# Strassen over 12 instead of 8 of the 16 chunks of an input projection, with the reloaded sums of x

## The chip, the cores and the metric

One core of one Trainium2 chip runs the kernel. The metric is the device time of one execution in microseconds (us). In the kernel text PE is TensorE, DVE is VectorE (`nc.vector`), ACT is ScalarE (`nc.scalar`), POOL is GpSimd, SP is SyncE, which here only issues DMAs.

## The reference, cut to what matters

One layer of a hybrid attention encoder in float32, for 16 meta tokens, 512 new frames of a prompt and 64 frames of a running stream (592 tokens, D_MODEL 2048):

```python
z = einsum('bld,dc->blc', h, w_in)            # h: 592 x 2048, w_in: 2048 x (52 tiles of 128 columns + 16 forget columns)
fox group: softmax(q k^T * SCALE + c_q - c_k, causal) v       # 16 heads, c is the running sum of log-sigmoid(forget gate)
swa group: sliding-window softmax with relative bias and a sink, 16 query heads on 4 key heads
out = concat(fox * silu(fg), swa * silu(sg)) @ w_out          # 2048 x 2048
y = layer_norm(ALPHA * x + out)
```

All keys, values and log forget values are outputs as well. The 52 column tiles of the input projection are the longest part of the kernel, and the change is in it.

## The kernel before, in words

**Precision.** Each float32 operand is split into a high part (a copy by ACT to float32r) and a low part (raw minus high, by DVE). A product of one 128-row chunk of the contraction is three matmuls: high x high, high x low, low x high. `xh`, `xl` hold x split once; `wh`, `wl` hold the split weights of the two tiles in work.

**Duos.** A duo is two column tiles (f = 0, 1) times two halves of the tokens (h = 0 `early`, h = 1 `late`, 296 tokens each; for gate and query tiles the first half is 280, as the meta tokens are left out). That is four results of 16 chunks each. The first tile pair ("v", "g") is projected plainly while x arrives (`opening_products`); then come duos 1 to 25. For the first `2 * CUT` chunks a duo is a 2 x 2 block product done in Strassen's way with seven block products instead of eight (`block_product`), each of `CUT` chunks; the remaining chunks are done plainly (`plain`). `CUT` is 4: seven block products of 4 chunks and eight plain units of 4 chunks, all in `UNITS` = 15 units of 12 matmuls (`unit`, u = 0 to 14). Every unit counts up `unit_done`. Banks TOP, BOTTOM and SIDE collect the products; DVE forms the results from them and from `first_part`, `diff_part`, `mid_part`, `last_part` (`take_six`, `take_seven`, `take_five`, `join`), ACT's `keep_first` frees TOP after unit 0.

**Sums.** The block products need sums of weight blocks, made for every duo by DVE (`make_seven`, `make_five`, `make_six`, `make_four`, each followed by a split into high and low: `seven_part`, `five_part`, `six_part`, `right_part`, `four_part`), and three sums of x blocks, made once in `opening_splits` (L1378 to L1382) and kept in SBUF split in high and low: `sum7`, `sum6`, `sum3`. `x21 - x22` is made in place at L1393. `front_parts` splits the FRONT (the first `2 * CUT` chunks) of tile 0, `back_parts` the BACK of either tile.

**Stretches.** `whole` writes the order out: a first duo alone; stretches of two duos ("vg", "qk") for each pair of fox heads; two longer stretches at the start of the two halves of the swa group; six short stretches of one duo ("gq"); and a final stretch in which the output projection (`out_step`) begins. While the duos of one pair are projected, the attention of the pair before is spread over the same steps s: `score_at`, `turn_at`, `value_at` of `Stretch` say before which step PE issues the five query tiles' scores, transposes of the probabilities, and products with the values. DVE handles `scores` at the same s and `reciprocals` two steps later, ACT `probabilities` one step later, `scale_rows` two later and `keep_turned` one after the transposes. `out_at` is where `gate_heads` (L1343) multiplies by the gates, `v_at` where the values of the next pair are transposed (`turn_values`, `keep_values`), `cached_at` where the cached keys are split. Every engine runs its own copy of this loop in order, so an instruction that waits holds up all that stands behind it on that engine.

**In the first duo** DVE also computes the forget gates: `gate_inputs`, `gate_ones`, `gate_reciprocals` (s = 3), `gate_logs` (s = 5), `gate_sums` (s = 7, the running sums, `c_ready`). PE's `turn_gates` transposes them behind unit GATES_TURNED_AT = 11, DVE's `keep_gates` reads them at s = 10 (the loop variable, after which PE's `turn_values` at s = V_FIRST_AT = 14 may overwrite the bank; it waits on `cq_ready`).

**Loads.** SP loads the weights of the next duos as FRONT and BACK pieces of both tiles (`load_part`, L596), 512 KB each, each as soon as DVE has made the low parts of what it overwrites. The POOL queue loads the row terms `cbc` (L728, L782), the cached keys and values, and stores the outputs and the finished pairs.

Of the kernel before, what the change touches and what calls it, by code (L numbers as in the profile page):

```python
# [24 lines left out]
F32 = mybir.dt.float32  # L25
# [39 lines left out]
UNITS = 15  # L65
DUOS = PROJ_TILES // 2
CUT = KO // 4
CUT_LEN = CUT * P
HALF = TOK // 2
GATES_TURNED_AT, V_FIRST_AT = 11, 14  # L70
GATE_ROWS = 80
BIAS_COPIES = FOX_PAIRS
RAW = 12
MIX_PARTS = [(0, 2), (2, 5), (5, 8), (8, 12), (12, 14)]
# [46 lines left out]
class Fox(Values):  # L121
# [31 lines left out]
    @staticmethod  # L153
    def metas(g, i):
        return 4 * g + i + 1


class Swa(Values):
# [32 lines left out]
    @staticmethod  # L191
    def metas(g):
        return 4 * FOX_PAIRS + g - FOX_PAIRS + 1
# [8 lines left out]
class Stretch:  # L202
# [8 lines left out]
    def __init__(self, duos, d0=None, own=None, pair=None, kv=None, kind=None, g=None, kvs=None,  # L211
# [5 lines left out]
        self.steps = OUT_STEPS if final else UNITS * len(duos)  # L217


        if final:  # L220
            score = [2 * i + 1 for i in range(5)]
        elif len(duos) == 2:
            score = [3 * i + 3 for i in range(5)]
        else:
            score = [2 * i + 1 for i in range(5)]
        turn = [x + 4 for x in score]
        value = [turn[2], turn[2], turn[4], turn[4], score[4] + 5 if len(duos) < 2 else score[4] + 7]
        self.score_at, self.turn_at, self.value_at = score, turn, value
        self.out_at = None if kind is None or keep else value[-1] + 2
        self.before_at = 0 if final else 2  # L230
        self.v_at = None
        if kv is not None:
            self.v_at = value[-1] + 3 if kind else V_FIRST_AT
        self.cached_at = self.steps - 5
# [55 lines left out]
def build(nc, xT, w_all, w_ff, b_f, lf_cache, k_cache, v_cache, sinks, rel, keep_k, keep_v,  # L290
          x_p, x_s, ln_g, ln_b, y_p, y_s, fkT, fvT, lf_out, skT, svT, kept_k, kept_v):
    ctx = ExitStack()
    with ctx:
# [10 lines left out]
        def sem(name):  # L304
# [8 lines left out]
        sum7_high, sum7_low, sum6_high, sum6_low, sum3_high, sum3_low = (  # L313
            sb(f"sum{n}", [P, CUT, HALF], F32R) for n in ("7_high", "7_low", "6_high", "6_low", "3_high", "3_low"))


        raw7, raw6, raw3 = (sb(f"raw{n}", [P, CUT, HALF], F32, at=sums_at + 4 * CUT * HALF * (2 * i + 1))
                            for i, n in enumerate((7, 6, 3)))
# [52 lines left out]
        gate_terms = sb("gate_terms", [P, 5, HALF], F32, at=keys_at)  # L371
        z, e, u1, wk, az = (gate_terms[0:GATE_ROWS, i, :] for i in range(5))
# [3 lines left out]
        cT = sb("cT", [N_HEADS, C_LEN], F32, at=keys_at + 5 * TOK * 4)  # L376
# [32 lines left out]

        c_rows = nc.dram_tensor("c_rows", [N_HEADS, C_LEN], F32, kind="Internal").ap()  # L410
        rel_rows = nc.dram_tensor("rel_rows", [N_HEADS, REL], F32, kind="Internal").ap()
        rel_copies = nc.dram_tensor("rel_copies", [N_HEADS, P, REL], F32, kind="Internal").ap()
# [12 lines left out]
        z_cleared = sem("z_cleared")  # L425
# [1643 lines left out]
```

## Time and profile before

| | |
|---|---|
| median of 3 runs | 1018.45 us (1018.03 to 1019.0) |
| profiled execution, its own time | 1019.1 us |
| its span in the profile | 1017.6 us |
| opening (x arrives, first pair "v", "g") | 0 to 39.25 us |
| duos 1 to 25 | 39.25 to 795.7 us |
| output projection and layer norm | to 1017.6 us |
| PE busy | 998.6 us (98%) |
| DVE busy | 715.2 us (70%) |
| ACT busy | 531.7 us (52%) |
| DMA | 115.06 MB, mean 113 GB/s |

The time of an execution is its span and some 1.5 us around it. "Busy" of PE is the union of overlapping matmuls (each shown as some 0.3 us although one follows another after about 0.14 us), so the pace is read from start times. The duos begin, in the timeline of PE, at 39.25 (duo 1), 67.29, 102.17, 129.91, 161.94, 189.68 and 221.62 us (duo 7); duo 18, the first short one, runs from 550.5 to 581.9, duo 19 to 613.4 us. In the rows of busy time by stretch the columns are: stretch, its length, busy time (and instructions) of PE, PEld, DVE, ACT and POOL, PE's granted clock, share of the DMA engines, GB/s. In a timeline row the first two numbers are start and duration.

### The profile page before, as it was taken

To read this page: it belongs to the slowest core of one execution; us is meant where nothing else is said; L and a number is where in the kernel's file an instruction comes from. 1 tells how busy PE (TensorE), PEld (TensorE's weight loads), DVE (VectorE), ACT (ScalarE), POOL (GpSimd) and SP (SyncE) were. 2 spreads that over 40 slices of the span, in tenths; PEclk is the share of its full clock that TensorE was granted. 3 is DMA by queue.
4 is the path that set the end of the run, shared out by engine and by line. 5 is a ranking of instruction groups with operands and counts; after the bars stand their busy time and mean duration, and the time that the engine had idled before them with its cause. 6 is when DMAs were issued, how large, how long until landed. Compare 5 with 4: busy or idle time off the path is not lost.

```text
span 1017.6 us, 20277 instructions
## 1 busy us (share of the span) xinstructions
PE 998.6 (98%) x7283; PEld 937.3 (92%) x7283; DVE 715.2 (70%) x1423; ACT 531.7 (52%) x1217; POOL 81.5 (8%) x156
## 2 busy tenths in 40 slices
PE   9999999999999999999999999999999999999995
PEld 6899999999999999999999999999999888888884
DVE  6988686776868677686767787668787655141685
ACT  5556465565645556464655676556677562111400
POOL 1620101001010100001010000000000000000000
PEclk9999999999999999999999999999999999999998
DMA  9142333223233323234321222231226443222423
GB/s 347 57 134 100 117 112 130 90 96 108 94 125 110 126 67 103 98 106 140 111 95 60 91 81 98 98 105 56 85 82 249 173 175 104 83 82 82 166 68 118
DMA packets 36258, 115.06 MB, mean 113 GB/s; under 512 B 9312, under 2 KB 9728, under 8 KB 33584
## 3 DMA queue, kind: packets, MB, share of 16 engines
q1 hardware_dynamic: 24208, 87.00, 24.8%
q0 software_dynamic: 11856, 27.14, 7.9%
q8 instruction: 31, 0.51, 0.2%
q10 hardware_dynamic: 144, 0.26, 0.1%
q14 instruction: 19, 0.16, 0.1%
HBM read 99.31 MB, written 18.29 MB: 116 GB/s over the span
## 4 chain that ended last, share of the span: by engine, by line
PE 86%; DVE 6%; DMA 4%; issue 2%; ACT 2%; SPq 1%; DVEq 0%; ACTq 0%
PE ps L1642 28%; PE ps L1652 25%; PE ps L1895 20%; PE ps L1860 5%; PE ps L1834 4%; DMA w_raw<-in_w_all 2%; PE ps L1818 2%; PE ps L1817 2%; DMA x_raw<-in_xT 2%; DVE wl L1118 1%; DVE tb L1295 1%; PE ps L1880 1%; SPq L582 0%; PE ps L1838 0%; ACT pt L961 0%
## 5 line engine op out<-in xcount | busy, mean ns | idle before, releaser
L1642 PE MATMUL ps<-xh,wh 128*128 128x296 f32 (+1 forms) x860 | 258.8, 301 | 0.2 <-DVE xl L1366 0.2
L1642 PE MATMUL ps<-xh,wl 128*128 128x296 f32 (+1 forms) x860 | 254.8, 296 | 0.0
L1642 PE MATMUL ps<-xl,wh 128*128 128x296 f32 (+1 forms) x860 | 254.6, 296 | 0.0
L1895 PE MATMUL ps<-wh,mix_parts 128*128 128x512 f32 x576 | 184.1, 390 | 0.0
L1642 PEld LDWEIGHTS ps<-xh,wh 128*128 128x128 f32 x860 | 161.8, 188 | 3.8 <-DVE xl L1366 1.8
L1642 PEld LDWEIGHTS ps<-xl,wh 128*128 128x128 f32 x860 | 161.9, 188 | 0.0
L1642 PEld LDWEIGHTS ps<-xh,wl 128*128 128x128 f32 x860 | 161.5, 188 | 0.0
L1118 DVE TENSOR_TENSOR wl<-w_raw,wh 128x1024 fp32r<-128x1024 f32 (+1 forms) x150 | 143.0, 953 | 19.8 <-ACT wh L853 8.5
L939 ACT ACTIVATE tb<-tb,small 128x256 f32<-128x256 f32 (+5 forms) x160 | 81.3, 508 | 92.2 <-DVE small L1314 64.2
L1895 PEld LDWEIGHTS ps<-wh,mix_parts 128*128 128x128 f32 x576 | 108.2, 188 | 22.3
L1895 PE MATMUL ps<-wl,mix_parts 128*128 128x512 f32 x320 | 124.5, 389 | 0.0
L1652 PE MATMUL ps<-xh,wh 128*128 128x296 f32 x400 | 121.4, 304 | 2.0 <-ACT first_part L891 1.4
L1652 PE MATMUL ps<-xl,wh 128*128 128x296 f32 x400 | 119.2, 298 | 0.0
L1652 PE MATMUL ps<-xh,wl 128*128 128x296 f32 x400 | 119.1, 298 | 0.0
L1652 PE MATMUL ps<-sum_high,wh 128*128 128x296 f32 x300 | 92.1, 307 | 1.2 <-DVE kT L1224 1.2
L1652 PE MATMUL ps<-sum_high,wl 128*128 128x296 f32 x300 | 89.7, 299 | 0.0
L1652 PE MATMUL ps<-sum_low,wh 128*128 128x296 f32 x300 | 89.6, 299 | 0.0
L1114 DVE TENSOR_TENSOR wl<-w_raw,wh 128x1024 fp32r<-128x1024 f32 x32 | 38.1, 1222 | 68.9 <-ACT wh L841 68.8
L1652 PEld LDWEIGHTS ps<-xh,wh 128*128 128x128 f32 x400 | 75.2, 188 | 2.6 <-ACT first_part L891 1.6
L951 ACT ACTIVATE tb<-tb,small 128x256 f32<-128x256 f32 (+4 forms) x160 | 71.7, 495 | 9.8 <-DVE small L1329 9.8
L1652 PEld LDWEIGHTS ps<-xl,wh 128*128 128x128 f32 x400 | 75.4, 189 | 0.0
L1652 PEld LDWEIGHTS ps<-xh,wl 128*128 128x128 f32 x400 | 75.2, 188 | 0.0
(198 smaller groups left out, 1737.3 us busy)
## 6 DMA issues: line engine op xcount, KB each, us to landing
w_raw<-in_w_all SPq DMA_DIRECT2D x106, 512.0 KB, 4.5
w_raw<-in_w_all SPq DMA_DIRECT2D x14, 1024.0 KB, 4.8
cbc<-c_rows POOLq DMA_DIRECT2D x16, 360.0 KB, 4.1
x_raw<-in_xT SPq DMA_DIRECT2D x7, 592.0 KB, 11.7
rows<-in_x_p POOLq DMA_DIRECT2D x4, 1024.0 KB, 5.2
out_y_p<-rows SPq DMA_DIRECT2D x16, 256.0 KB, 2.5
mix_rows<-mixT POOLq DMA_DIRECT2D x14, 288.0 KB, 2.4
rel_copies<-rel_rows POOLq DMA_DIRECT2D x8, 384.0 KB, 10.5
```

The costliest lines, as they stand in the source:

```text
L939: nc.scalar.activation(t, t, ACT.Exp, bias=nm, accum_out=total[:, i % 3, head:head + 1]).then_inc(exp_done, 1)
L951: nc.scalar.activation(row, row, ACT.Copy, scale=recip[:, i % 3, head:head + 1]).then_inc(scaled, 1)
L1114: nc.vector.tensor_tensor(wl[slot][:, a], w_raw[slot % 2][:, a], wh[slot][:, a].bitcast(F32), ALU.subtract).then_inc(w_low, 1)
L1118: nc.vector.tensor_tensor(low, raw, high.bitcast(F32), ALU.subtract).then_inc(done, 1)
L1295: ins = nc.vector.scalar_tensor_tensor(out=rows_[:, head, a:b], in0=st.score_out(ps, head, piece, b - a), scalar=cqp[:, i, head:head + 1], ...
L1642: ins = nc.tensor.matmul(ps[:, bank, result(tile, h)], a[f][:, w], b[:, ko, first:first + width], start=(ko == n_first and i == 0), stop=( ...
L1652: ins = nc.tensor.matmul(ps[:, bank, 0:HALF], a[:, w], b[:, j, :], start=(start and j == 0 and i == 0), stop=(stop and j == CUT - 1 and i ...
L1817: nc.tensor.matmul(out, queries, k2[:, head, a:b], start=True, stop=False)
L1818: ins = nc.tensor.matmul(out, queries, k_low[:, head, a:b], start=False, stop=True)
L1834: ins = nc.tensor.transpose(st.turn_out(ps, head, j), tb[:, i % SLOTS, head, first:first + P], ident[:])
L1860: ins = nc.tensor.matmul(ps[head_rows(head), bank, at:at + q], v_nat[:, block_, HD * head:HD * head + HD], moving[:, head, 0:q], start=(j ...
L1895: ins = nc.tensor.matmul(ps[:, bank, :], a, b[slot][:, w], start=(ko == 0 and i == 0), stop=(ko == KO - 1 and i == len(products) - 1))
```

## The change

- `CUT` is 6: Strassen covers 12 chunks, and `REST` = 2 chunks remain for each plain unit. The steps of a duo are 29 pieces of 2 chunks (6 matmuls) instead of 15 units of 4 chunks; `unit_done` still counts 15 per duo. The plain units of result (0, 1) now stand ahead of those of (1, 0): units 9 and 10 are (0, 1), units 11 and 12 are (1, 0).
- The sums of x are half as large again, and only `sum7` stays in SBUF. `sum6` and `sum3` share the tile `sum_both` (1776 KB, high and low). Both are stored in DRAM once in the first duo (`sum_rows`) and each is loaded again for each duo: `sum6` when unit 7 is done, `sum3` when unit 1 is done. `sum3` is now made in place of x11 in `x_raw`, and split in the first duo by `last_sum`.
- FRONT of a tile is 768 KB, BACK 256 KB; the weight sums are 768 columns.
- Scores in a stretch of two duos stand at pieces 10, 16, 22, 28, 34 (before, in units: 3, 6, 9, 12, 15); in a short one at 1, 5, 9, 13, 17 (units 1, 3, 5, 7, 9). ACT and DVE follow with a lag of 2 and 4 pieces. Transposes come 8 pieces after the scores.
- Several steps of ACT and DVE move, `back_parts(d, 0)` of DVE from the end of the duo before to piece 2, the join of (1, 0) to piece 27. In the first duo the gates' steps stand at s = 14, 14 and 18, `turn_gates` at 25, `keep_gates` at 26, `turn_values` at 28.
- The copies of the bias rows in DRAM are made for 32 instead of 128 rows, and read in four DMAs instead of two.

```diff
+UNIT_PIECES = [3, 3, 3, 3, 1, 1, 3, 3, 3, 1, 1, 1, 1, 1, 1]
+PIECES = sum(UNIT_PIECES)
-CUT = KO // 4
+CUT = 3 * KO // 8
+REST = (KO - 2 * CUT) // 2
-GATES_TURNED_AT, V_FIRST_AT = 11, 14
+GATES_TURNED_AT, V_FIRST_AT = 25, 28
...
-            score = [3 * i + 3 for i in range(5)]
+            score = [6 * i + 10 for i in range(5)]
         else:
-            score = [2 * i + 1 for i in range(5)]
-        turn = [x + 4 for x in score]
+            score = [4 * i + 1 for i in range(5)]
+        self.lag = 1 if final else 2
+        turn = [x + 4 * self.lag for x in score]
...
@@ sync @@
             for f in range(2):
-                sp.wait_ge(w_low, f + 1)
+                sp.wait_ge(w_low, f + 3)
                 load_part(1, f, FRONT, front_loaded)
             for f in range(2):
-                sp.wait_ge(w_low, f + 3)
                 load_part(1, f, BACK, back_loaded)
+            sp.wait_ge(sum_low, 2)
+            sp.dma_start(sum_rows[0], sum_both[:].rearrange("p a b c -> p (a b c)")).then_inc(sums_stored, 16)
             sp.wait_ge(back_low[0], 1)
             load_part(2, 0, BACK, back_loaded)
+            sp.wait_ge(sum_low, 4)
+            sp.dma_start(sum_rows[1], sum_both[:].rearrange("p a b c -> p (a b c)")).then_inc(sums_stored, 16)
+            sp.wait_ge(sums_stored, 32)
...
-                sp.wait_ge(*((four_made, d) if f == 0 else (right_low, d)))
+                sp.wait_ge(*((four_made, d) if f == 0 else (five_low, d)))
...
+            def load_sums(i, used, loaded):
+                sp.wait_ge(unit_done, used)
+                sp.dma_start(sum_both[:].rearrange("p a b c -> p (a b c)"), sum_rows[i]).then_inc(loaded, 16)
+            def load_three(d):
+                load_sums(1, UNITS * (d - 1) + 2, three_loaded)
+            def load_duo(d):
+                load_next_front(d, 0)
                 load_next_front(d, 1)
-                load_next_front(d, 0)
                 load_next_back(d)
+                load_sums(0, UNITS * (d - 1) + 8, six_loaded)
                 sp.wait_ge(back_low[0], d + 1)
                 load_part(d + 2, 0, BACK, back_loaded)
+            load_duo(1)
+            with sp.Fori(2, DUOS - 1) as d:
+                load_three(d)
+                load_duo(d)
+            load_three(DUOS - 1)
...
@@ vector, opening_splits @@
-                nc.vector.tensor_tensor(raw3[:], x12, raw6[:], ALU.subtract).then_inc(sum_made, 1)
+                dve.wait_ge(gates_summed, 1)
+                nc.vector.tensor_tensor(x11, x12, raw6[:], ALU.subtract).then_inc(sum_made, 1)
...
                 six_part(1)
+                gate_inputs()
                 nc.vector.tensor_tensor(x21, x21, x22, ALU.subtract).then_inc(sum_made, 1)
-                gate_inputs()
-                dve.wait_ge(sum_high, 3)
-                low_of(sum3_low[:], raw3[:], sum3_high[:], sum_low)
                 gate_ones()
                 back_parts(1, 0)
...
@@ vector, run @@
                     if inside:
-                        if u == 2:
+                        if r == 2 and not st.first:
+                            back_parts(d, 0)
+                        if r == 6:
                             take_six(st, k)
+                            five_part(d)
+                        if r == 8:
+                            right_part(d)
+                        if r == 9:
                             take_seven(st, k)
+                            make_four(d, (unit_done, st.after(k, 2)))
+                        if r == 14:
                             join(st, k, 0, 0)
+                        if r == 17:
                             take_five(st, k)
+                        if r == 25:
+                            join(st, k, 0, 1)
+                        if r == 27:
                             join(st, k, 1, 0)
...
+                        if st.first and r == 10:
+                            last_sum()
+                        if r == 12:
                             back_parts(d, 1)
+                        if r == 14:
                             four_part(d)
                         if not last:
+                            if r == 20:
                                 front_parts(d + 1)
+                            if r == 21:
                                 make_seven(d + 1, (unit_done, st.after(k, 7)))
                                 make_five(d + 1)
+                            if r == 22:
                                 make_six(d + 1)
+                            if r == 25:
                                 seven_part(d + 1)
                                 six_part(d + 1)
...
@@ tensor, unit @@
                 elif u == 1:
+                        else:
+                            pe.wait_ge(side_summed, d - 1)
+                            pe.wait_ge(six_loaded, 16 * d - 16)
+                        pe.wait_ge(six_low, d)
+                    ins = block_product(piece, SIDE, of_tile(1, A), (both_high, both_low), True)
...
                 elif u == 7:
+                        if st.first:
+                            pe.wait_ge(sum_low, 4)
+                        else:
+                            pe.wait_ge(three_loaded, 16 * d - 16)
```

In ACT's loop `front_parts(d + 1)` stands at piece 18, `seven_part` and `six_part` at 24, the evacuations of the results at 14, 25 and 27.

## Rows read from the trace of the kernel before

**Rows 1.** The page, part 1: busy time and share of each engine

```profile
PE 998.6 (98%) x7283; PEld 937.3 (92%) x7283; DVE 715.2 (70%) x1423; ACT 531.7 (52%) x1217; POOL 81.5 (8%) x156
```

**Rows 2.** Busy time by stretch: duos 1, 2, 6 and 19

```profile
39.25:67.29 28.04, 26.02 (x194) 25.31 (x192) 25.89 (x45) 13.32 (x26) 12.06 (x32) 1.00 0.36 122
67.29:102.17 34.88, 32.95 (x261) 31.68 (x262) 28.23 (x59) 22.71 (x49) 2.21 (x3) 1.00 0.31 103
189.68:221.62 31.94, 31.94 (x264) 31.53 (x262) 25.64 (x53) 19.46 (x45) 2.19 (x3) 1.00 0.33 111
581.93:613.36 31.43, 31.43 (x261) 30.51 (x260) 24.82 (x57) 21.97 (x61) 1.77 (x3) 1.00 0.24 82
```

**Rows 3.** All waits of PE from 135 to 760 us

```profile
PE ps L1834 <- ACT tb L951: 1.7, 3, 1.1
```

**Rows 4.** Timeline of PE, duo 19: a matmul and the ninth behind it

```profile
588.14 0.30 PE L1652 MATMUL ps<-xh,wh 128*128 128x296 f32 x1
...
589.36 0.29 PE L1642 MATMUL ps<-xh,wh 128*128 128x280 f32 x1
```

**Rows 5.** Timeline of PE, opening: from here six matmuls of 280 columns

```profile
18.12 0.30 PE L1642 MATMUL ps<-xh,wh 128*128 128x280 f32 x1
...
18.89 0.30 PE L1642 MATMUL ps<-xh,wh 128*128 128x296 f32 x1
```

**Rows 6.** Groups of DVE by form: busy, mean ns

```profile
L1118 DVE TENSOR_TENSOR wl<-w_raw,wh 128x1024 fp32r<-128x1024 f32 x75 | 91.5, 1221 | 16.5 <-ACT wh L853 8.5 <-ACT wh L847 8.0
L1118 DVE TENSOR_TENSOR wl<-w_raw,wh 128x512 fp32r<-128x512 f32 x75 | 51.4, 686 | 3.3
...
L1118 DVE TENSOR_TENSOR sum_low<-raw,sum_high 128x1184 fp32r<-128x1184 f32 x3 | 4.1, 1387 | 0.0
```

**Rows 7.** Groups of ACT by form

```profile
L847 ACT ACTIVATE wh<-w_raw 128x1024 fp32r<-128x1024 f32 x25 | 26.4, 1058 | 8.2 <-DMA w_raw<-in_w_all 6.2 <-PE ps L1652 1.9
...
L859 ACT ACTIVATE wh<-w_sum 128x512 fp32r<-128x512 f32 x25 | 15.7, 626 | 2.2 <-DVE w_sum L1134 1.8
```

**Rows 8.** Timeline of DVE in the opening and duo 1

```profile
26.72 1.38 DVE L1378 TENSOR_TENSOR raw<-x_raw 128x1184 f32<-128x1184 f32 x1
...
47.73 1.99 DVE L1428 RECIPROCAL gate_terms<-gate_terms 80x296 f32<-80x296 f32 x1
...
58.48 1.19 DVE L1118 TENSOR_TENSOR wl<-w_raw,wh 128x1024 fp32r<-128x1024 f32 x1
...
63.02 0.23 DVE L1461 COPY cq<-ps 128x64 f32<-128x64 f32 x1
```

**Rows 9.** Timeline of PE: where it stood idle in duo 1

```profile
45.73 0.41 PE L1652 MATMUL ps<-xh,wh 128*128 128x296 f32 x1 [1.37 <-ACT first_part L891]
...
67.29 0.41 PE L1652 MATMUL ps<-xh,wh 128*128 128x296 f32 x1 [0.65 <-DVE mid_part L1224]
```

**Rows 10.** DMA issues from 70 to 72.5 us: KB each, us to landing

```profile
w_raw<-in_w_all SPq DMA_DIRECT2D x1, 512.0 KB, 3.5
```

**Rows 11.** DMA issues from 846 to 848 us

```profile
w_raw<-in_w_all SPq DMA_DIRECT2D x1, 1024.0 KB, 4.8
```

**Rows 12.** Busy time by stretch around and behind the last matmul

```profile
1003.00:1006.00 3.00, 3.00 (x15) 2.49 (x14) 0.79 (x2) 0.00 (x0) 0.00 (x0) 1.00 0.88 309
1006.00:1009.00 3.00, 1.36 (x7) 0.79 (x5) 1.53 (x3) 0.00 (x0) 0.00 (x0) 1.00 0.00 0
1009.00:1012.00 3.00, 0.00 (x0) 0.00 (x0) 2.90 (x7) 0.29 (x1) 0.00 (x0) 0.68 0.00 0
1012.00:1017.00 5.00, 0.00 (x0) 0.00 (x0) 2.67 (x5) 0.00 (x0) 0.00 (x0) 0.50 0.58 210
```

**Rows 13.** Timeline of ACT in duo 6: tile 2 of the scores scaled

```profile
208.08 1.11 ACT L951 ACTIVATE tb<-tb,small 128x384 f32<-128x384 f32 x2
```

**Rows 14.** Timeline of PE in duo 6: that tile's score and its transposes

```profile
200.42 0.34 PE L1817 MATMUL ps<-k,q 128*128 128x400 f32 x1
...
208.96 0.72 PE L1834 MATMUL ps<-ident,tb 128*128 128x128 f32 x5
```

More of the change, by code:

```diff
@@ L1049, in run @@
-                        if u == 10:
-                            evacuate(st, k, 1, 0)
-                        if u == 11 and not last:
-                            seven_part(d + 1, (unit_done, st.after(k, 10)))
-                            six_part(d + 1, (unit_done, st.after(k, 7)))
-                        if u == 13:
-                            evacuate(st, k, 0, 1)
+                        if r == 24 and not last:
+                            seven_part(d + 1, (unit_done, st.after(k, 8)))
+                            six_part(d + 1, (unit_done, st.after(k, 7)))
@@ L1066, in run @@
+                    for i in st.at(st.score_at, s - 2 * st.lag):
                         scale_rows(st, i)
+                    if inside and r == 18 and not last:
+                        front_parts(d + 1, (unit_done, st.after(k, 6)))
                     if st.kv is not None and s == st.cached_at:
@@ L1478, in run @@
                 for s in range(st.end + 1):
-                    k, u = divmod(s, UNITS)
+                    k, r = divmod(s, PIECES)
                     inside = k < len(st.duos)
                     ready = None
-                    for i in st.at(st.score_at, s - 2):
+                    if inside:
+                        d, last = st.duo(k), st.last and k == len(st.duos) - 1
+                    for i in st.at(st.score_at, s - 2 * st.lag):
                         reciprocals(st, i)
-                    if u == 0 and 1 <= k <= len(st.duos):
+                    if r == 0 and 1 <= k <= len(st.duos):
                         join(st, k - 1, 1, 1)
@@ L1541, in run @@
                         keep_values(st)
-                    if st.first and s == GATES_TURNED_AT - 1:
+                    if st.first and s == GATES_TURNED_AT + 1:
                         keep_gates()
@@ L1686, in unit @@
                 elif u == 3:
-                    pe.wait_ge(first_kept, d)
-                    ins = block_product(TOP, of_tile(0, B), of_x(second_x, early), True, False)
+                    if begins:
+                        pe.wait_ge(first_kept, d)
+                    ins = block_product(piece, TOP, of_tile(0, B), of_x(second_x, early), False)
                 elif u in (4, 5):
@@ L1715, in unit @@
                         pe.wait_ge(under_made, d)
-                    ins = plain(1, 1, duo[1], BOTTOM, range((u - 11) * CUT, (u - 10) * CUT), 2 * CUT)
-                ins.then_inc(unit_done, 1)
+                    ins = plain(1, 1, duo[1], BOTTOM, rest(u - 13), 2 * CUT)
+                if piece == UNIT_PIECES[u] - 1:
+                    ins.then_inc(unit_done, 1)
             def opening_products():
```

284 lines of the change are left out of this document (145 added, 139 removed).

## The prediction

> **What bounds the kernel now.** I read the busy times first: PE is busy for 98% of the span, DVE for 70%, ACT for 52% [rows 1]. Then the waits of PE: between 135 and 760 us it waits for another engine for 1.7 us in all, each time for ACT's scaled probabilities [rows 3]. So the projection runs at the pace of PE's own instructions, and what the change takes off PE is worth its full price as long as the others keep up. Then the busy time by duo, to see how near they are: in duo 6, which carries scores, DVE is busy 25.64 of 31.94 us, in the short duo 19 it is 24.82 of 31.43, and ACT 21.97 [rows 2]. In duo 1 DVE is the limit: 25.89 of 28.04 us, and PE idles for ACT and DVE at 45.73 and 67.29 [rows 2, 9].
>
> **Matmuls saved.** A duo has 180 matmuls before (7 x 4 x 3 = 84 in block products, 8 x 4 x 3 = 96 plain), 174 after (126 + 48). Nine of 296 columns take 589.36 - 588.14 = 1.22 us, 0.136 us each [rows 4]; six of 280 columns take 18.89 - 18.12 = 0.77 us, 0.128 each [rows 5]. The 42 new ones all have 296 columns, the 48 that go are partly of 280: 12 of them in a "vg" or "qk" duo, 24 in a "gq" duo. That is 12 x 0.128 + 36 x 0.136 - 42 x 0.136 = 0.72 us saved, or 0.62 us in the six "gq" duos. Nineteen duos at 0.72 and six at 0.62 give **17.4 us**. The order of the units and the cut of units into pieces add no PE instruction.
>
> **What DVE and ACT get.** A 1024-column subtraction takes 1.221 us, one of 512 columns 0.686 [rows 6]: 1.045 ns a column and 0.15 us fixed. Per duo FRONT grows by 512 columns, two BACKs shrink by 512 each, nine operations on sums grow by 256: 1792 columns, **+1.87 us** of DVE. ACT pays 0.84 ns a column (1.058 against 0.626 us) [rows 7]; it splits FRONT, two BACKs and five sums, so +768 columns, +0.65 us. Both lie beside PE's work. Duo 6 becomes 27.5 of about 31.2 us for DVE, duo 19 26.7 of 30.8: no longer loose. If that cover goes, each microsecond of lateness is PE's.
>
> **Where a scored tile now stands.** From the score of tile 2 in duo 6 to its transposes PE takes 208.96 - 200.42 = 8.54 us [rows 14]; ACT's two scalings run from 208.08 to 209.19 [rows 13], so the second head is ready just as PE comes to it. After, the distance is 8 pieces of 6 matmuls, the same 48 matmuls, but ACT has in front of those scalings a FRONT copy 0.43 us longer, and DVE a `four_part` 0.27 longer. I take 0.3 us lost in each of the seven fox duos with scores. In a short stretch the query half of (1, 0) is joined at piece 27, the score that needs it is at piece 1 of the next duo. PE does 4 pieces between (3.3 us) and the last values; DVE has to finish `seven_part` and `six_part` (1.9 us), join (296 columns, 0.46), wait for ACT's copy and subtract: about as long. I take 0.4 us in six short duos. Waits there before may go in exchange (1.7 us [rows 3]); together **+2 us**, bounds 0 and 14 (1 us in each of the 14 duos with scores).
>
> **The reloaded sums.** 512 KB land in 3.5 us, 1024 KB in 4.8 [rows 10, 11]: 1.3 us for 512 KB and 2.2 fixed, so 1776 KB about 6.7 us and 768 KB 4.2. `sum3` is asked for at piece 6 and needed at piece 17: 11 x 0.82 = 9.0 us and what PE does of the attention. `sum6` has pieces 20 to 32, 9.8 us. The queue order on SP is right for it: the FRONTs come behind `sum3` and are wanted only at piece 18 and 21. I cost both at nothing; the cover is the 2.3 us or more between landing and use.
>
> **The first duo.** Here I follow DVE. Before, it takes up the sums of x at 26.72 and is at the gates' reciprocal at 47.73 [rows 8]. After, up to the end of `last_sum`: eight operations on x sums with 592 more columns, 0.62 each, +5.0; weight parts +1.6 (FRONT +0.54, six sums +1.6, BACK -0.54); `right_part` and `make_four`, which move ahead, +1.8; the wait for ACT's Tanh, behind a longer copy of x, +1.2. So `last_sum` ends at about 57.4. Only then does SP store the second sum, and it waits for the landing (`sums_stored` 32) **ahead of the FRONT loads of duo 2**: 57.4 + 6.7 for the store (taken as for a load; no row has a large store) + 0.5 issue + 4.2 for FRONT 0 = 68.8, ACT's copy of 1536 columns 1.5, 70.3. DVE is done with the gates' sums at 66.7 (before, 58.48 - 47.73 = 10.75 us from the reciprocal to the FRONT of duo 2 [rows 8]; less `right_part` and `make_four` 1.25, less 0.26 for a smaller BACK and a larger `four_part`, behind 57.4). After FRONT's copy it has, in order, FRONT 1.7, three sums 3.0, join 0.46, `seven_part`, `six_part` 1.9, the queries' low parts 0.9, cached keys 0.6, `keep_gates` 0.3: 79.2, where this copy started at 63.02 before [rows 8]. PE's `turn_values` at s = 28 waits for just this (`cq_ready`), and PE gets there at about 68.7 (unit 7 from 57.5 on, units 7 to 10 at 18 and 6 matmuls each 6.5 us, `turn_gates` behind the gates' sums at 66.7, two pieces): it would stand **idle for some 10 us**. Then the values' transposes 0.6 and the last piece 0.8: duo 2 begins at 80.6 and not at 67.29 [rows 9], **13.3 us later**. On the way PE waits in short pieces for `six_low`, `first_kept`, `mid_part`, `sum3` and `c_ready`, which that start already holds. Bounds: with no delay by the store DVE alone gives 77; with a store twice as slow 87. In duo 2 the lateness is partly regained: its 34.88 us become 31.94 - 0.72 = 31.2 (DVE catches up before piece 6), **-3.7 us**. The duos' own 1.44 us of saving are inside these two.
>
> **The clock.** In the only long idle time of PE in this trace, behind the last matmul (start 1006.98 us), the granted clock is 1.00 up to 1009, 0.68 in the mean of 1009 to 1012 and 0.50 behind [rows 12]: it falls from 2.4 to 1.2 GHz about 2.7 us after PE stops. I expect the same in the long wait of duo 1. What it costs to come back no row shows; if the slow state lasted as long as the fall took, 2.7 us at half pace lose 1.4. I take **+1 us**, bounds 0 and 3. The Trainium skill ("TensorE: Matmul & The Clock Gate", section "HAM oscillation — how this bites in real kernels") says that an idle gap between bursts of matmuls drops the array to its half rate and that the transition is then paid again; rows 12 agree with the first half, and the second is not to be seen before. It speaks against this change, and here it would touch one gap, not every duo.
>
> **Sum.** 1019.1 (this execution's own time, span 1017.6) + 13.3 - 3.7 - (17 x 0.72 + 6 x 0.62 = 16.0 in duos 3 to 25) + 1 + 2 = 1015.7. The execution is 0.65 above the median of the runs, so **1015.0 us**. Nothing moves in the output projection: the first halves of its weights come at pieces 20 and 28, as early as before.
>
> **Rivals.** (a) *DVE becomes the bound* in the 14 duos with scores: slower. For it: 26.7 of 30.8 us with the forced waits between ACT and DVE on top, and the short distance from piece 27 to the next score. Against it: the 2 to 3 us in which DVE idles at a short duo's end now. At 0.8 us lost in each, 11 instead of 2, the time is 1024; it decides from 0.54 us each (1020.5). (b) *`sum3` arrives late* in fox duos where `cbc` (720 KB) shares the DMA engines: 1776 + 720 KB need about 8.5 us, slack 0.5 us or more by rows 10 and 11; at half a microsecond late in 9 to 16 duos, 5 to 8 us more, about 1021. (c) *The opening is cheaper and the tight chains hold*: DVE's path alone (77), no stall in the scored duos, no clock loss: 1015.0 - 3.6 - 2 - 1 = 1008.4. (d) *The clock stays at half pace* for longer than it took to fall, 3 us lost instead of 1: 1017. This is the case in which the page's rule, told above, counts most.
>
> **How the numbers follow.** Forecast 0.41 (1011 to 1018), (a) 0.20, (b) 0.10, (c) 0.22, (d) 0.07. A measurement of this kernel can tell about 0.2%, 2 us, from no change: faster means under 1016.4, slower above 1020.5. Faster: (c) and three quarters of the forecast, with a little of (d): 0.55. Slower: (a) nearly whole and half of (b): 0.24. Within: 0.21. The range runs from the middle of (c) to the middle of (a): 1008 to 1024.
>
> **What would show it.** Right: 174 matmuls a duo and 0.7 us less in the plain duos; a gap of 8 to 12 us of PE ahead of the values' transposes in duo 1, released by DVE's copy of the gates; duo 2 starting near 80; a granted clock under 1 in that stretch; a store of 1776 KB landing in about 6.7 us. Wrong: PE waits of over 0.5 us at the transposes, the first score or `sum_both` in duo after duo, or a duo 2 that starts before 75.

## The result, and the profile after

The changed kernel takes 1076.0 us (median of 4 runs, 1073.97 to 1077.34) beside 1018.7 (1018.03 to 1019.64) for the kernel before: ratio 1.056, 95% interval 1.054 to 1.058. The forecast was 1015.0, the range 1008 to 1024: wrong, and on the other side. The profiled execution took 1075.05 us, its span is 1073.5.

The page of the changed kernel, part 1; it answers to [rows 1]:

```profile
PE 1007.0 (94%) x7133; PEld 938.1 (87%) x7133; DVE 767.0 (71%) x1423; ACT 545.1 (51%) x1217; POOL 89.0 (8%) x172
```

PE issues 150 matmuls less, as forecast, and falls from 98% to 94% of a longer span. The waits of PE over the whole span (engine, line, what it waited for: us in total, times, longest) show where it stands:

```profile
PE ps L1952 <- DVE mixT L1394: 29.6, 7, 4.8
PE ps L1952 <- DVE cq L1518: 9.2, 1, 9.2
PE ps L1889 <- DVE k_low L1311: 6.3, 2, 3.6
PE ps L1889 <- issue: 2.1, 1, 2.1
PE ps L1932 <- ACT pt_meta L999: 2.1, 4, 0.6
PE ps L1858 <- DVE tb L1505: 1.8, 1, 1.8
```

Between 135 and 760 us there were 1.7 us of waits before [rows 3]. Now one line alone has 29.6: L1952, the first transpose of `turn_values`, seven times, once in the second duo of each fox stretch (duos 3, 5, ... 15), until DVE has done L1394, `gate_heads`. Busy time by stretch, duos 1, 2, 5 and 19:

```profile
38.96:79.80 40.84, 27.31 (x187) 25.91 (x186) 35.81 (x54) 19.22 (x31) 15.23 (x39) 0.90 0.51 192
79.80:109.01 29.21, 29.21 (x211) 28.97 (x211) 22.29 (x41) 15.71 (x32) 1.25 (x2) 0.96 0.58 211
173.82:210.90 37.08, 32.34 (x261) 30.66 (x261) 25.42 (x51) 18.68 (x44) 3.26 (x6) 0.95 0.53 195
629.06:660.70 31.64, 31.05 (x256) 29.88 (x255) 26.61 (x57) 22.13 (x62) 2.72 (x5) 1.00 0.57 197
```

Against [rows 2]: duo 1 is 12.8 us longer, duo 2 is 5.7 shorter. In duo 5 PE is busy for only 32.34 of 37.08 us, while DVE is busy for 25.42, as in duo 6 before, and idle for 11.7: its load alone doesn't say why PE waits. (Duo 5 itself had 18.77 of 27.74 us on DVE before; as the work was moved between the duos, that is no like for like.) Where the 56 us came from, by the starts of the duos in the trace; the last column is the version that the experiments end with:

| stretch, us | before | after | forecast (without its 3 us for clock and tight tiles) | e8 |
|---|---|---|---|---|
| start of duo 2 | 67.29 | 79.80 | 80.6 | 71.68 |
| duos 2 and 3 | 62.62 | 65.87 | 58.2 | 61.99 |
| duos 4 to 15 (six fox stretches) | 360.26 | 388.91 | 351.6 | 359.40 |
| duos 16 and 17 | 60.35 | 58.76 | 58.9 | 59.78 |
| duos 18 to 25 | 245.22 | 255.18 | 240.1 | 252.89 |
| rest | 221.87 | 224.93 | 221.9 | 223.34 |

Above the forecast stand 45 us in duos 2 to 15, 15 in duos 18 to 25 and 3 in the rest: at the start of the output projection PE waits 2.1 us instead of 0.7, and runs at a granted clock of 0.60 for 2.9 us behind that.

**The chain in duo 5.** From the DMA issues between 183 and 189 us (KB each, median us from issue to landing), the timeline of ACT, the timeline of DVE, and that of PE:

```profile
sum_both<-sum_rows SPq DMA_DIRECT2D x1, 1776.0 KB, 9.9
w_raw<-in_w_all SPq DMA_DIRECT2D x2, 768.0 KB, 9.6
cbc<-c_rows POOLq DMA_DIRECT2D x2, 360.0 KB, 9.6
```

```profile
196.77 1.49 ACT L885 ACTIVATE wh<-w_raw 128x1536 fp32r<-128x1536 f32 x1 [3.31 <-DMA w_raw<-in_w_all]
198.17 1.25 ACT L966 ACTIVATE k<-kc 64x128 fp32r<-64x128 f32 x4
```

```profile
199.45 0.58 DVE L1311 TENSOR_TENSOR k_low<-kc,k 64x128 fp32r<-64x128 f32 x2 [4.79 <-ACT k L966]
200.07 1.76 DVE L1167 TENSOR_TENSOR wl<-w_raw,wh 128x1536 fp32r<-128x1536 f32 x1
201.74 0.95 DVE L1183 TENSOR_TENSOR w_sum<-w_raw 128x768 f32<-128x768 f32 x1
202.80 0.96 DVE L1189 TENSOR_TENSOR w_raw<-w_raw,w_raw 128x768 f32<-128x768 f32 x1
203.79 0.96 DVE L1195 TENSOR_TENSOR w_raw<-w_raw,w_sum 128x768 f32<-128x768 f32 x1
204.67 0.81 DVE L1394 SCALAR_TENSOR_TENSOR mixT<-ps,mixT 128x512 f32 x2
```

```profile
205.63 0.37 PE L1952 MATMUL ps<-ident,v_twice 128*32 128x128 f32 x1 [4.74 <-DVE mixT L1394]
```

Read it from the end. PE stood ready at 200.9 and waited for `gate_heads`, because the transposes go into PSUM banks of which `gate_heads` reads one. `gate_heads` is three pieces late in the list of DVE: at piece 52 it stands behind FRONT's low half and the three sums of weights (pieces 49 to 51), 4.6 us of work. DVE in turn had been idle for 4.79 us, since the cached keys' copies stand on ACT behind FRONT's copy, and that had been idle for 3.31 us for FRONT itself. (The change moved these copies too, `cached_at`: before, they stood at unit 25 of 30, behind `gate_heads`; now they are at piece 48, and cost this chain 1.25 us on ACT and 0.6 on DVE.) FRONT 0 had landed 8.9 us after its issue (187.8 to 196.7), while `sum3`, two FRONTs and the row terms `cbc` shared the DMA engines. A late transfer of 768 KB thus crossed two engines and reached a transpose that has nothing to do with it. What each link is worth is for the experiments.

**The clock**, from busy time by stretch (the granted clock is the third number from the end), around that wait:

```profile
200.90:205.60 4.70, 0.00 (x0) 0.01 (x1) 4.56 (x7) 1.58 (x2) 0.00 (x0) 0.95 0.46 193
205.60:207.00 1.40, 1.37 (x7) 1.36 (x8) 1.30 (x3) 1.01 (x3) 0.54 (x1) 0.50 0.00 0
207.00:208.00 1.00, 1.00 (x6) 1.00 (x5) 0.97 (x2) 0.00 (x0) 0.00 (x0) 0.50 0.50 194
208.00:209.00 1.00, 1.00 (x8) 1.00 (x7) 0.95 (x4) 0.00 (x0) 0.00 (x0) 0.72 0.27 101
209.00:210.00 1.00, 1.00 (x10) 1.00 (x9) 1.00 (x5) 0.00 (x0) 0.00 (x0) 1.00 0.00 0
```

From 2.4 to 1.2 GHz and back: behind the wait PE runs some 3 us at half pace, so a wait of 4.7 costs 4.7 + 1.4. From the first transpose to the next duo the seven fox stretches take 5.3 to 6.0 us, and 3.9 where nothing waited (duo 17): 1.4 to 2.1 us each. Duo 5 without the wait takes 30.80 us (e8), with it 37.08: 6.3. The seven waits cost 29.6 + 11.4 = 41 us in all.

### The profile page after: what moved, and what is told of

Read it like the earlier page. It is cut to its first block, busy times and chain, and to the rows that moved or that the text cites. A ratio compares the mean times of both kernels' runs of the same rounds, so it can differ in the third digit from the quotient of the medians.

```text
span 1073.5 us, 20086 instructions
## 1 busy us (share of the span) xinstructions
PE 1007.0 (94%) x7133; PEld 938.1 (87%) x7133; DVE 767.0 (71%) x1423; ACT 545.1 (51%) x1217; POOL 89.0 (8%) x172
## 4 chain that ended last, share of the span: by engine, by line
PE 52%; DVE 19%; ACT 9%; issue 8%; DMA 7%; DVEq 1%; ACTq 0%; SPq 0%
PE ps L1967 19%; PE ps L1708 17%; PE ps L1698 8%; DMA w_raw<-in_w_all 6%; DVE wl L1167 4%; ACT tb L975 3%; PE ps L1932 2%; DVE tb L1346 2%; PE ps L1906 2%; DVE w_sum L1201 2%; DVE small L1365 1%; DVE w_sum L1183 1%; ACT wh L885 1%; ACT k L966 1%; PE ps L1889 1%
## 5 line engine op out<-in xcount | busy, mean ns | idle before, releaser
L1708 PE MATMUL ps<-xh,wh 128*128 128x296 f32 x600 | 183.1, 305 | 1.2 <-ACT first_part L927 0.8
L1708 PE MATMUL ps<-xh,wl 128*128 128x296 f32 x600 | 181.1, 302 | 0.0
L1708 PE MATMUL ps<-xl,wh 128*128 128x296 f32 x600 | 180.5, 301 | 0.0
L1167 DVE TENSOR_TENSOR wl<-w_raw,wh 128x1536 fp32r<-128x1536 f32 (+1 forms) x150 | 147.7, 998 | 15.9 <-ACT wh L885 12.0
L1698 PE MATMUL ps<-xh,wh 128*128 128x296 f32 (+1 forms) x460 | 145.6, 316 | 0.0
L1698 PE MATMUL ps<-xl,wh 128*128 128x296 f32 (+1 forms) x460 | 140.3, 305 | 0.0
L1698 PE MATMUL ps<-xh,wl 128*128 128x296 f32 (+1 forms) x460 | 140.0, 304 | 0.0
L1708 PE MATMUL ps<-sum_both,wh 128*128 128x296 f32 x600 | 127.9, 304 | 1.3 <-DVE wl L1167 1.2
L1708 PEld LDWEIGHTS ps<-sum_both,wh 128*128 128x128 f32 x600 | 97.3, 190 | 2.4 <-issue 1.4
L1708 PE MATMUL ps<-sum_both,wl 128*128 128x296 f32 x300 | 89.8, 299 | 0.0
```

What stands on the lines that cost most here:

```text
L1167: nc.vector.tensor_tensor(low, raw, high.bitcast(F32), ALU.subtract).then_inc(done, 1)
L1698: ins = nc.tensor.matmul(ps[:, bank, result(tile, h)], a[f][:, w], b[:, ko, first:first + width], start=(ko == n_first and i == 0), stop=( ...
L1708: ins = nc.tensor.matmul(ps[:, bank, 0:HALF], a[:, w], b[:, j, :], start=(j == 0 and i == 0), stop=(stop and j == CUT - 1 and i == 2))
```

## The experiments

Each is the changed kernel with the edit shown. In the expectations, a "pair" is a fox stretch of two duos, and PE's own work in it is put at 58.6 us (58.8 to 58.9 by the starts of the duos, see the matmuls below). All but e11 were timed in one execution each, beside one of the kernel before (1018.2 to 1019.1 us). Four executions of the changed kernel lie within 3.4 us, four of e11 within 2.6, so a difference under 4 us between two versions is not shown by their times.

**e1: `gate_heads` ahead of FRONT.**

```diff
-        self.out_at = None if kind is None or keep else value[-1] + 2 + 2 * (not final)
+        self.out_at = None if kind is None or keep else value[-1] + (2 if final else 1)
-        self.cached_at = self.steps - (10 if kind else 4)
+        self.cached_at = self.steps - (3 if kind else 4)
```

> Edit: in the stretches of two duos DVE multiplies the heads by the gates at step 49, ahead of its low part of FRONT, and the cached keys are split at step 55 instead of 48. Nothing else moves. Theory L (late FRONT): in the changed kernel PE waits 3.6 to 4.8 us ahead of the values' transposes in seven fox stretches, because gate_heads stands on DVE behind the cached keys and FRONT, and these behind ACT's copy of a FRONT that lands 9 us after its issue; the granted clock then falls to 0.50 for some 3 us. Then these seven waits go, each pair of duos falls from about 64.5 to about 58.5 us, and the time from 1076 to 1030 (plus or minus 5). Rival V (DVE has too much work): the wait only moves to the next use of DVE's results, and the time stays above 1060. Rival C (the transposes wait for something else than gate_heads): no change, 1076.

1051.2 us: 25 less, where 46 were expected. The waits of PE from 100 to 860 us:

```profile
PE ps L1708 <- DVE kT L1275: 6.8, 7, 1.6
PE ps L1708 <- DMA sum_both<-sum_rows: 5.9, 6, 1.6
PE ps L1889 <- DVE k_low L1311: 5.7, 2, 3.2
PE ps L1932 <- ACT pt_meta L999: 3.6, 6, 1.2
```

All waits at L1952 are gone. Two smaller kinds stand in their place, both in the first duo of the stretch: the second unit waits for the join of kT, and unit 7 for `sum3`. The edit has two parts, as `gate_heads` at piece 49 would still stand behind the cached keys at 48; e5 has the first without the second. The order was the largest part, but it had also covered a lateness of the transfers.

**e2: POOL's row terms later.** The two loads of `cbc` for the next pair (720 KB) go behind POOL's loads of cached keys and values.

```diff
-                if st.own is Fox:
-                    pool.wait_ge(score_read, Fox.base(g))
...
+                    if st.own is Fox:
+                        pool.wait_ge(score_read, Fox.base(g))
...
                     if not st.keep:
                         store_mixed(st.g)
```

> Edit: POOL issues the two loads of the row terms cbc (720 KB) of the next fox pair behind the loads of the cached keys and values, after step 48, and not at step 36, where they share the DMA engines with the reload of sum3 and the FRONTs. Theory L with the DMA engines as its cause: FRONT 0 of the second duo lands 4 to 5 us earlier than the 8.9 us after issue seen in duo 5, the wait ahead of the values' transposes falls from 4.2 to under 1 us, the clock stays at 1.00, time 1030 to 1040. If the sum reload alone makes it late: FRONT lands some 6 us after issue, wait 1 to 2 us, time 1045 to 1055. Rival V (DVE's work): landing earlier changes nothing, 1076.

**e3: half of each reload.** Only the high half of a sum is loaded, 888 KB for 1776.

```diff
-                sp.dma_start(sum_both[:].rearrange("p a b c -> p (a b c)"), sum_rows[i]).then_inc(loaded, 16)
+                sp.dma_start(sum_both[:, 0, :, :].rearrange("p b c -> p (b c)"), sum_rows[i][:, 0:CUT * HALF]
+                             ).then_inc(loaded, 16)
```

> Edit: each reload of a sum of x brings only its high half (888 instead of 1776 KB); the low half is left as it stands, so part of the products uses wrong low parts. Theory L: FRONT 0 lands about 2.2 us earlier (888 KB at 2.5 us per 1024 KB), the wait in the fox stretches falls from 4.2 to about 2 us, and with it the fall of the clock goes: 7 x (2.2 + 2.2) less, about 1045. Rival V: 1076. If it falls below 1035, the reloads cost more than their place in the queue.

1059.4 and 1053.1 us. The waits at L1952 were 17.0 us in e2 and 16.4 in e3, with the same seven places:

```profile
PE ps L1952 <- DVE mixT L1394: 17.0, 7, 2.9
```

```profile
PE ps L1953 <- DVE mixT L1395: 16.4, 7, 3.0
```

Both fell short of their theory L (1030 to 1040, and 1045). In duo 5 FRONT 0 lands 7.1 us after its issue in e2 and 7.0 in e3, against 8.9: 1.8 us sooner, not 4 to 5. Taking 720 KB out of the way of FRONT, or 888 KB, takes about 1.8 us from each wait. Waits of 1.8 to 3.0 us are left in both: neither load alone makes the wait. The two were not taken away together in this order.

**e4: in the first duo, FRONT of duo 2 ahead of the second store.**

```diff
-            sp.wait_ge(sum_low, 4)
-            sp.dma_start(sum_rows[1], ...).then_inc(sums_stored, 16)
-            sp.wait_ge(sums_stored, 32)
...
                 load_next_front(d, 0)
                 load_next_front(d, 1)
+                if first:
+                    sp.wait_ge(sum_low, 4)
+                    sp.dma_start(sum_rows[1], ...).then_inc(sums_stored, 16)
+                    sp.wait_ge(sums_stored, 32)
```

> Edit: in the first duo SP issues both FRONT loads of duo 2 ahead of the second store of the sums, and waits for the stores only then. The prediction's chain: store 6.7 us, then FRONT; without it DVE's own work decides: duo 2 starts at about 76.5 instead of 79.8 us, the wait ahead of the first values' transposes falls from 9.2 to about 6 us, time 1073. Rival (the store is not on the path, DVE alone): duo 2 starts at 79.8 as before, 1076.

1069.0 us. PE's wait in duo 1 fell from 9.24 to 6.42 us and duo 2 starts at 78.7: the store was worth 2.8 us of the wait. Duo 1 itself began 2.0 us later in this execution (at 40.99), so duo 2 starts 1.1 us sooner and not 3.3. Of the 7 us gained the rest is scattered: 2.6 us less at L1952, and 1.6 in the output part, where PE waits the same 2.1 us but the clock stays at 1.00 behind it.

**e5: the scores back.** The scores of a long stretch began at unit 3 before, behind 36 matmuls, and at piece 10 after, behind 60. Here they begin at piece 6, behind 36 again: everything of the attention in a long stretch stands four pieces sooner, and `gate_heads` (48) is ahead of FRONT (49) again.

```diff
-            score = [6 * i + 10 for i in range(5)]
+            score = [6 * i + 6 for i in range(5)]
```

> One part of the change undone: in the long stretches the five scores begin at piece 6 again and not at piece 10, and all of the attention behind them comes four pieces sooner with them; the gates' heads (piece 48) then stand ahead of the next FRONT (piece 49) on DVE, and the values' transposes are at piece 50. Theory L (the 5 us a pair come from the order alone: transposes behind a gates operation that stands behind a late FRONT): the wait of 3.6 to 4.8 us and the half clock behind it vanish in all seven fox pairs, a pair takes about 60 us instead of 65, and the time is 1076 - 7 x 5.5 = about 1038. Theory Q (DVE and ACT lack capacity, the wait is only where that shows): as much as in the run in which the gates' heads alone went ahead, pairs of 61.5 to 62 and 1050, with the wait for kT's join at the start of a pair in its place. The first duo (starts of duo 2 at 79.8) and duos 18 and 23 stay as they are in both.

1046.2 us, 30 less than the changed kernel: one number in the plan accounts for more than half of the loss. The waits from 100 to 860 us:

```profile
PE ps L1889 <- DVE k_low L1311: 13.7, 9, 3.7
PE ps L1932 <- ACT pt_meta L999: 2.2, 5, 0.6
PE ps L1708 <- DVE kT L1275: 2.2, 3, 0.8
```

It lies between the two theories: no wait at L1952 from 100 us on, and a fox stretch takes 60.9 us (duos 4 to 15, 365.55), but seven of the nine waits for the low half of the keys are new, 0.95 to 1.2 us each: this is what the later scores had avoided.

**e6: e1, e2 and e4 together.**

> Three edits together: the gates' heads ahead of FRONT, POOL's row terms behind its other loads, and in the first duo FRONT's loads ahead of the second store of the sums. Theory L: each took a separate delay away, so what is left of sum3's lateness (0.6 to 1.6 us a pair) goes too; pairs of 60 us, 1051 - 7 x 1.2 - 1.5 = about 1041. Theory Q: what remains is DVE's backlog at the start of a pair (join of kT, 0.5 to 1.6 us), which no order of loads mends; pairs stay at 61.5, 1049.

**e7: with the values' transposes at piece 50.**

```diff
-            self.v_at = value[-1] + 6 if kind else V_FIRST_AT
+            self.v_at = value[-1] + 2 if kind else V_FIRST_AT
```

> As the three edits together, and the values' transposes, with DVE's five copies of them, at piece 50 of a fox stretch instead of 54, so that DVE has 1.3 us less to do just ahead of the joins at pieces 56 and 58. Theory L: the waits for kT's join at the start of a pair (0.5 to 1.6 us) shrink by about 1 us each and the first score of duos 18 and 23 waits 2 us instead of 3: some 6 + 2 us below the run with three edits, about 1033. Theory Q: DVE makes up the same time between two FRONTs, the wait only moves; within 2 us of the run with three edits.

1036.2 and 1034.9 us. e6 came out 5 us under the expectation of theory L: fox stretches of 60.3 us, no wait for kT in them, duo 2 at 76.95. But one part of that theory failed: the waits for `sum3` did not go, they are 6.0 us in six stretches (5.9 in e1). Theory Q is out for the step from e1 to e6: the load of DVE and ACT is the same in these kernels, and an order mended the waits. e7 gained 1.3 us where its theory L had 8: the waits for kT that it should have shortened were gone in e6 already. Its time alone doesn't tell it from e6.

**e8: DVE copies the turned gates sooner in the first duo.** `keep_gates` right behind FRONT's low half (piece 20) instead of at piece 26.

```diff
                             if r == 20:
                                 front_parts(d + 1)
+                                if st.first:
+                                    keep_gates()
...
-                    if st.first and s == GATES_TURNED_AT + 1:
-                        keep_gates()
```

> On top of the version with three edits and the values' transposes at piece 50 (1034.9 us): in the first duo DVE copies the turned gates right behind FRONT's low half (piece 20) and not behind the seven low halves, sums and joins that follow it (piece 26). Theory O (the 6 to 9 us of PE's idle time ahead of the values' transposes are only an order on DVE): the wait falls by 5 us or more, duo 2 starts near 71, waits 1 to 2 us at its second unit for the low half of six, and ends 4 us sooner: 1031. Theory D (DVE is busy without a break from 25 to 77 us, the opening is bound by its work): duo 2 starts sooner, but the wait only moves into it, to the joins and to six_low; duo 3 starts at 105 to 106 as before, 1034 to 1035.

1030.6 us. PE's wait for DVE ahead of the values' transposes is gone; it waits 2.40 us for POOL instead, and 1.5 us inside duo 2. Duo 2 starts at 71.7 (77.5 in e7), duo 3 at 103.0 (106.3): theory O. The same two copies of 0.2 us each, in another place, are worth 3 to 4 us (3.3 by the start of duo 3). The waits from 100 to 860 us that are left:

```profile
PE ps L1889 <- DVE k_low L1311: 4.7, 2, 2.4
PE ps L1932 <- ACT pt_meta L999: 3.2, 5, 1.1
PE ps L1708 <- DMA sum_both<-sum_rows: 2.3, 4, 0.8
PE ps L1889 <- issue: 2.1, 1, 2.1
PE ps L1906 <- ACT tb L987: 0.9, 3, 0.4
```

**e9: the cached keys one piece later** (on top of e8).

```diff
-        self.cached_at = self.steps - (3 if kind else 4)
+        self.cached_at = self.steps - (2 if kind else 4)
```

> On top of that: ACT's four copies of the cached keys (1.24 us) and DVE's two (0.57) stand behind the join and the split of the new keys' first half, not ahead of them (piece 56 of 58 instead of 55). Theory B (the first score of duos 18 and 23 waits 2 us for the backlog of both engines): each of the two waits shrinks by 0.6 to 1.5 us, the time by 1 to 3 us, and nothing changes in the fox pairs. Rival: the join is itself late by the end of PE's unit 12, and the wait stays at 2 us.

1048.7 us, 18 slower than e8: a miss of both. The timelines of ACT and of DVE at the seam of duos 3 and 4:

```profile
136.29 0.63 ACT L891 ACTIVATE wh<-w_raw 128x512 fp32r<-128x512 f32 x1
136.83 1.25 ACT L966 ACTIVATE k<-kc 64x128 fp32r<-64x128 f32 x4
```

```profile
134.88 0.96 DVE L1311 TENSOR_TENSOR k_low<-kT,k 64x296 fp32r<-64x296 f32 x2 [0.52 <-ACT k L953]
138.12 0.58 DVE L1311 TENSOR_TENSOR k_low<-kc,k 64x128 fp32r<-64x128 f32 x2 [2.28 <-ACT k L966]
138.73 0.47 DVE L1275 TENSOR_TENSOR kT<-ps,last_part 128x296 f32<-128x296 f32 x1
```

ACT's copies slid behind four copies of new keys and BACK's, so DVE waited 2.28 us for them with the last join of the duo behind it. That join came at 138.7, against 136.6 in e8, PE's third unit waited for it (0.7 to 0.9 us in each of seven stretches), everything behind was late, and `sum3` later still (10.7 us of waits for it from 100 to 860 us, 2.3 in e8).

**e10: the scores of the short stretches one piece later** (on top of e9), which undoes "one sooner"; the last values stay at piece 28.

```diff
-            score = [4 * i + 1 for i in range(5)]
+            score = [4 * i + 2 for i in range(5)]
-                 score[4] + (5 if final else 11 if len(duos) < 2 else 14)]
+                 score[4] + (5 if final else 10 if len(duos) < 2 else 14)]
```

> On top of that, the other part of the change's attention undone: in the short stretches the scores stand one piece later (2, 6, 10, 14, 18) and the transposes with them, the last values stay at piece 28. Theory B: the waits at the first score of duos 18 and 23 shrink by up to 0.82 us each, but the last values come two pieces behind their transposes instead of three, and their wait of 0.6 us (four or five duos) becomes 1.4: +3 to +4 us against -1.6, so 1 to 3 us slower than with scores at piece 1. Rival: the last wait is not bound by that distance, and the time falls by 1.6.

1065.1 us, 16 slower than e9. The wait that grows is at the last values:

```profile
PE ps L1932 <- ACT pt L997: 16.6, 9, 2.8
```

The waits at the first scores of duos 18 and 23 shrank by 0.8 and 1.4 us, as theory B had it. But the six short duos take 34.1 to 40.1 us instead of 31.6 to 37.3. Scores one piece sooner thus earn their place: with two pieces between the last transposes and their values instead of three, PE waits there 2.8 us instead of 0.6, far more than the 0.8 of one piece. Moving the last values along as well wasn't tried.

**e11: the cached keys at piece 51** (on top of e8), and **e12: e8 with half of each reload**.

```diff
-        self.cached_at = self.steps - (3 if kind else 4)
+        self.cached_at = self.steps - (7 if kind else 4)
```

> On top of the version with DVE's copy of the turned gates at piece 20 (1030.6 us): the cached keys' copies (ACT 1.24 us, DVE 0.57 us) at piece 51 of a fox stretch instead of 55, behind FRONT's copy and ahead of the joins. Theory B (the first scores of duos 18 and 23 wait 2.3 us each for a backlog that ends in the new keys' low half): the two waits fall by 0.5 to 1.2 us each, the fox pairs keep their 59.9 us, 1028.5 to 1030. Rival (the order of the copies feeds back into the next pair, as when they went one piece later and every first duo of a pair took 1.9 us more): the pairs move by more than that, and then the pace of the pairs is set by what stands around their seam, not by the attention.

> On top of the version at 1030.6 us: each reload brings only the high half of a sum, 888 KB for 1776; the low halves stay those of the sum loaded last, so the output is not the reference's. Theory T (what is left over a pair of 58.6 us, the work that PE has, is 0.7 at the transposes and the rest in sum3's lateness): waits for sum3 vanish and the pairs take 59.3 us, 59.9 before, the time 1026 to 1028. Rival (with the order mended the DMA engines have room, and the reloads cost nothing, as forecast): pairs stay within 0.2 us of 59.9, the time within 2 us of 1030.6.

e11: 1033.2 us (median of 4, 1032.15 to 1034.7), 1.4% above the kernel before (ratio 1.0144, interval 1.0127 to 1.0161): no better than e8. The wait in duo 18 fell from 2.3 to 1.5 us, that in duo 23 did not move, and the fox stretches kept 59.9 us. The rival is out; theory B holds for one of its two waits, and its 1028.5 to 1030 was not reached.

e12: 1030.4 us, e8 1030.6. In part 6 of the pages of e12 and of e8:

```profile
sum_both<-sum_rows SPq DMA_DIRECT2D x48, 888.0 KB, 5.3
```

```profile
sum_both<-sum_rows SPq DMA_DIRECT2D x48, 1776.0 KB, 8.5
```

The reload lands 3.2 us sooner, the waits for it are gone, and the six fox stretches take 359.47 us, with the whole reload 359.40: with the order mended the reloads cost nothing there, and theory T is out. In e3, with the order as changed, the same edit gave 23 us. The DMA engines set how late FRONT was, and the order on DVE decided whether that mattered.

No version here beats the kernel before; the best is e8, 12 us above it. By the table, its first duo is 4.4 us longer than before and duos 18 to 25 are 7.7; its fox stretches are 0.9 us shorter in all six together. What would mend duos 18 and 23 wasn't found.

## Why the prediction was wrong

- **Matmuls saved: the count right, the time smaller.** 174 a duo. Duos 16 and 17, in which PE waits for nothing in the changed kernel, take 58.76 us, and the fox stretches 58.9 without their waits and the half clock behind them; duos 4 and 5 took 59.8 before. That is 0.9 us saved of 1.44 forecast; a short duo without its wait of 0.6 us takes 31.05 for 31.43, 0.4 of 0.62. Scaled up to all duos, an estimate, some 10 of the 17.4 us came. Both kinds of product follow one another after 0.136 us in the median, as the forecast had it; where the rest went was not followed.
- **DVE and ACT: right in size.** FRONT's low half takes 1.76 us for the 1.76 that the slope of [rows 6] gives, the sums 0.96. DVE is busy for 26.61 us in duo 19, 26.7 forecast.
- **The first duo: right, step by step.** `last_sum` ended at 56.06 (57.4), its store landed in 5.9 us (6.7), FRONT's low half began at 68.0 (70.3), `keep_gates` at 76.64 (79.2), PE idled 9.24 us (some 10), duo 2 began at 79.80 (80.6). Duo 2 regained 5.7 us and not 3.7. But the price was read as a fact of the sizes. By e8 (duo 2 at 71.7) 8 of the 12.5 us are order: the store ahead of FRONT (e4), and two small copies behind ten other operations.
- **The reloaded sums: this step failed.** The forecast gave the FRONTs 4.2 us each, as if alone, and no cost: "the FRONTs come behind `sum3` and are wanted only at piece 18 and 21". The reloads landed in 8.1 us in the median (6.7 forecast), in duo 5 in 9.9, and FRONT 0 in 8.9. At 4.2 it would have been there at 192.0, before ACT was free for it at 193.5; it came at 196.7. Rival (b) saw `cbc` on the same engines but looked for the wait at `sum3`; what came late was the transfer queued behind it.
- **The moved `gate_heads`: the step that failed most.** Under "Where a scored tile now stands" the forecast followed PE's distance from score to transposes, took 0.3 us a fox duo, and costed the four pieces at nothing elsewhere; the runs showed 3.6 to 4.8 us of wait in each of seven fox stretches. It never asked what `gate_heads` at piece 52 is now queued behind on DVE. In the timeline of DVE of the kernel before, duo 5, it starts as soon as FRONT's low half ends, and FRONT was in time:

```profile
176.70 1.22 DVE L1118 TENSOR_TENSOR wl<-w_raw,wh 128x1024 fp32r<-128x1024 f32 x1
177.84 0.82 DVE L1343 SCALAR_TENSOR_TENSOR mixT<-ps,mixT 128x512 f32 x2
```

  After, three sums stand between the two, the cached keys stand ahead of FRONT's low half, and FRONT is late. The order is worth 25 us in e1, with the cached keys moved as well, and 30 in e5; waits and half clock together are 41.
- **The clock: priced for one gap.** Forecast +1 us in one place. Duo 1 ran at half pace for 5.0 us behind its wait, 2.5 lost, and the seven fox waits cost 11.4 on top of themselves: some 14 us. The Trainium skill ("TensorE: Matmul & The Clock Gate", section "HAM oscillation — how this bites in real kernels") says that a wait repeated in every step makes the array go back to half rate each time and pay the transition again; the trace agrees for the seven waits of 3.6 to 4.8 us, at 1.4 to 2.1 us each; shorter ones did not always pay (below). Rival (d) applied it to one gap only.
- **Tight tiles: too small.** Forecast 0.4 us in six short duos. Duos 18 and 23 wait 2.7 and 3.6 us for the keys' low half: there the stretch before is "vg", "qk", and the tile joined at piece 27 is k, with four copies of ACT before the first score, not q. Even in e8 these two duos take 4.4 us more than the forecast's 30.8, the other short ones 0.8.

Rival (a) had the right sign with the wrong cause: PE did wait for DVE, and DVE had 5 us of slack in duo 5 (25.42 us of the 30.80 that it takes without the wait). What was wrong was the place of one operation in its queue.

## What to carry to other kernels

When a change moves an operation on an in-order engine, list what now stands ahead of it there, and what each of those waits for: an operation of 0.8 us behind a copy of a late load inherits all of that load's lateness. Slack in busy time says nothing about it; the distance between two neighbours in one queue does. And a wait of PE that recurs is priced with the half clock behind it.

## What the runs showed of the hardware

- A short wait can have its half clock behind it. In e2, busy time by stretch, two waits of PE (the first and third row) and the time after each:

```profile
511.20:513.20 2.00, 0.06 (x1) 0.01 (x1) 1.97 (x5) 0.79 (x2) 0.00 (x0) 1.00 1.02 426
513.20:516.20 3.00, 2.98 (x14) 2.96 (x15) 2.85 (x5) 1.00 (x3) 0.55 (x1) 0.52 0.88 348
386.10:388.50 2.40, 0.04 (x1) 0.00 (x0) 2.37 (x5) 1.19 (x2) 0.00 (x0) 1.00 0.98 407
388.50:391.50 3.00, 2.96 (x23) 2.99 (x24) 2.85 (x5) 1.01 (x3) 0.55 (x1) 1.00 0.83 330
```

  The clock is 1.00 in both waits. Behind the one of 2.0 us it is 0.52 for 3 us, behind the longer one of 2.4 us it stays at 1.00. Of the 14 waits of this kind in e2 and e3, seven (1.97 to 2.97 us) have a half clock behind them and seven (1.80 to 2.65) have none. So the length of a wait doesn't settle its price, and [rows 12] (a fall 2.7 us after the last matmul) was no safe bound from below.
- The 52 loads of 768 KB landed in 7.6 us in the median, beside the reloads and POOL's loads; the slope of [rows 10, 11] gives 4.2. In e8 they took 7.5 as well, and no wait of PE from 100 to 860 us is put down to them. The Trainium skill ("DMA: Bandwidth & Descriptors", section "Issuing engines are not separate DMA queues") says that transfers started by different engines run on the same DMA engines and interleave; e2 agrees: moving POOL's 720 KB helped loads that SP had issued.
